# Two transformer blocks in one kernel: orders, waits and small products at the passages between stages

## What is computed

```python
def first_block(x, ...):
    x = x + 0.5 * swiglu(rmsnorm(x, g_ffn1), w1_gate, w1_up, w1_down)      # ffn1, 2816 hidden
    p = rmsnorm(x, g_mix) @ w_in
    qa, ka, va, qi, ki, wi, cq, ckv, kr = jnp.split(p, split_points, axis=-1)
    ...                                # rotary positions on qa, ka, qi, ki and parts of cq, kr
    out_a = dsa_sparse_attention(qa, ka, va, qi, ki, wi)     # top 128 keys chosen by an index score
    out_b = mla_attention(cq, ckv, kr, ...)                  # latents normed, then 8 causal heads
    x = x + jnp.concatenate([out_a, out_b], axis=-1) @ w_out
    x = x + 0.5 * swiglu(rmsnorm(x, g_ffn2), w2_gate, w2_up, w2_down)      # ffn2
    return rmsnorm(x, g_final)

def second_block(x, c, ctx, c_ctx, ...):
    ml = jnp.split(silu(c) @ w_mod + b_mod, 9)               # modulation of x
    mc = jnp.split(silu(c_ctx) @ w_mod + b_mod, 9)           # and of the context
    x = x + 0.5 * ml[2] * swiglu_2(modulate(rms_norm(x, norm1_g), ml[0], ml[1]), ...)   # ffn3
    cx = cx + 0.5 * mc[2] * swiglu_2(modulate(rms_norm(cx, norm1_g), mc[0], mc[1]), ...)
    ...                                # norm2, w_in_2: convolution branch, 8 query and 2 key heads
    x = x + ml[5] * merge_branches(y_conv, o_l, gates, w_branch_conv, w_branch_attn, w_out)
    x = x + 0.5 * ml[8] * swiglu_2(modulate(rms_norm(x, norm3_g), ml[6], ml[7]), ...)   # ffn4
    return rms_norm(x, final_g)
```

## Time and profile before

| | us |
|---|---|
| median of 3 runs | 2712.87 |
| lowest and highest | 2710.14, 2714.3 |
| profiled execution, whole | 2712.72 |
| its span from the first to the last instruction | 2710.9 |

### The profile page before, as it was taken

How to read it: one execution, slowest core, us unless ns; L and a number is a source line. 1 busy time by engine, 2 the same in 40 slices (tenths; PEclk the granted TensorE clock), 3 DMA queues, 4 the chain that set the end, 5 groups by cost and what they waited for, 6 DMA issues and landing times.

```text
span 2710.9 us, 32788 instructions
## 1 busy us (share of the span) xinstructions
PE 2637.7 (97%) x12170; PEld 2105.8 (78%) x12170; DVE 1332.3 (49%) x2039; ACT 758.4 (28%) x1035; POOL 372.5 (14%) x274
## 2 busy tenths in 40 slices
PE   8999999998999999999999999999999999999998
PEld 6888877754468888878888888888887658888887
DVE  7666674577647665572222222444226653433334
ACT  4111132255622221241111111323322452321223
POOL 2111120000012010142102102202000003210102
PEclk9999999889899999999999999999999999999999
DMA  6444443200054444432122121232332002233331
GB/s 189 140 140 144 140 127 77 57 16 1 1 155 139 139 140 140 128 103 64 63 62 62 62 62 51 59 108 78 93 112 68 16 1 93 78 100 93 102 89 66
DMA packets 358031, 241.18 MB, mean 89 GB/s; under 512 B 14768, under 2 KB 356144, under 8 KB 357936
## 3 DMA queue, kind: packets, MB, share of 16 engines
q1 hardware_dynamic: 357936, 239.92, 30.0%
HBM read 237.79 MB, written 2.10 MB: 88 GB/s over the span
## 4 chain that ended last, share of the span: by engine, by line
PE 90%; DVE 4%; ACT 3%; issue 1%; DMA 1%; POOL 0%; SPq 0%; DVEq 0%; ACTq 0%; POOLq 0%
PE PS L716 23%; PE PS L723 22%; PE PS L718 22%; PE PS L698 4%; PE PS L701 4%; PE PS L699 4%; PE PS L1121 2%; PE PS L1101 1%; PE PS L895 1%; PE PS L977 1%; PE PS L970 1%; PE PS L950 1%; PE PS L655 1%; DVE VA L1501 1%; PE PS L1112 1%
## 5 line engine op out<-in xcount | busy, mean ns | idle before, releaser
L716 PE MATMUL PS<-NH,WH 128*128 128x512 f32 (+1 forms) x2128 | 621.1, 373 | 10.7 <-DVE WL L1477 3.8
L718 PE MATMUL PS<-NH,WL 128*128 128x512 f32 (+1 forms) x2128 | 619.0, 372 | 0.0
L723 PE MATMUL PS<-NL,WH 128*128 128x512 f32 (+1 forms) x2128 | 590.7, 372 | 0.0
L1477 DVE TENSOR_TENSOR WL<-RAW,WH 128x2048 fp32r<-128x2048 f32 x190 | 468.7, 2467 | 106.7 <-ACT WH L1149 106.3
L1149 ACT ACTIVATE WH<-RAW 128x2048 fp32r<-128x2048 f32 x190 | 363.8, 1915 | 527.9 <-PE PS L723 494.2
L716 PEld LDWEIGHTS PS<-NH,WH 128*128 128x128 f32 x2128 | 386.4, 188 | 82.6 <-issue 9.8
L723 PEld LDWEIGHTS PS<-NL,WH 128*128 128x128 f32 x2128 | 388.9, 189 | 72.0 <-POOL NL L2076 0.4
L718 PEld LDWEIGHTS PS<-NH,WL 128*128 128x128 f32 x2128 | 388.6, 188 | 71.6
L1223 ACT ACTIVATE SA<-PS 128x512 f32<-128x512 f32 x104 | 62.2, 599 | 628.9 <-PE PS L723 595.6
L716 PE MATMUL PS<-HH,WH 128*128 128x512 f32 (+1 forms) x820 | 238.1, 371 | 0.0
L718 PE MATMUL PS<-HH,WL 128*128 128x512 f32 (+1 forms) x820 | 237.8, 371 | 0.0
(11 more groups left out here) (305 smaller groups left out, 2602.0 us busy)
## 6 DMA issues: line engine op xcount, KB each, us to landing
RAW<-in_ffn_w_in SPq DMA_DIRECT2D x88, 512.0 KB, 5.0
MW<-in_w_mod SPq DMA_DIRECT2D x72, 512.0 KB, 3.5
RAW<-in_w_in SPq DMA_DIRECT2D x70, 512.0 KB, 4.4
RAW<-in_w_gate SPq DMA_DIRECT2D x44, 512.0 KB, 4.1
RAW<-in_w_up SPq DMA_DIRECT2D x44, 512.0 KB, 5.3
RAW<-in_w_down SPq DMA_DIRECT2D x32, 512.0 KB, 4.4
RAW<-in_ffn_w_out SPq DMA_DIRECT2D x32, 512.0 KB, 4.0
RAW<-in_w_out SPq DMA_DIRECT2D x16, 512.0 KB, 4.5
```

What stands on the lines that cost most here:

```text
L716: pe.matmul(outs[half][x], w[half][0], xh(k), start=k == 0, stop=False)
L718: pe.matmul(outs[half][x], w[half][1], xh(k), start=False, stop=False)
L723: last = pe.matmul(outs[half][x], w[half][0], xl(k), start=False, stop=k == kn - 1)
L1477: dve.tensor_tensor(WL[1 - s][:, :], RAW[1 - s][:, :], WH[1 - s][:, :].bitcast(F32), ALU.subtract).then_inc(w_lo, 1)
```

## The change

- Norms: the diagonals go. The inverse root itself, a column read 128 times (`spread`), is the stationary operand and `ident` the moving one. This holds for the final norm of the first block too, where GpSimd made the diagonals.
- w_in: the weights of stage 1 are asked for ahead of the constants, and VectorE's wait for the constants stands behind the first split.
- Tail stages: VectorE adds the first half's residual ahead of the split.
- Modulation: the last four stages of ffn1, the stages of `w_out` and the last two chunks of ffn2 carry none; 30 stages of ffn3 do, with sums in CXIN. The fold has three parts in place of two, and its last is finished behind the convolution.
- w_out and w_branch_attn: the first stage begins with the four k that are ready and waits for `at_o` (`at2_o`) in its middle. SyncE waits for `at_o` only before the context's loads.
- First attention: the mask instruction gives the negated value and its minimum, so the negation goes and exp takes scale -1. From unit 48 on VectorE multiplies in place of ScalarE.
- The memset before the convolution clears the two edge columns alone.

```diff
-        M0 = {"ffn1": 0, "wo": NF + 12, "ffn2": NF + 12 + KD // 2}
-        assert M0["ffn2"] + NF + 12 == 2 * MOD_PAIRS
+        M0 = {"ffn1": 0, "ffn2": NF + 8, "ffn3": NF + 20}
         NCTX = 5 * KD
...
+        def last_mods(name, c):
+
+            return {("ffn1", 2): 1, ("ffn3", 2): 1, ("ffn2", 0): 2}.get((name, c), 0)
...
+        def spread(r, t):
+
+            return r[:, t:t + 1].to_broadcast([P, P])
...
+        BY_ACT = 48
...
                             sp.dma_start(MW[t][:, :, :], mod_weights(t, 0)).then_inc(mod_loaded[t], 16)
                     return
                 t = (s + b0) % 2
-                if m0 == M0["wo"]:
-                    sp.wait_ge(at_o, NG)
                 if not (isinstance(j, int) and j + m0 < 2):
                     sp.wait_ge(mod_s, j * 8 + 8 * (m0 - 1))
...
-                if n == 0:
+                if n == 1:
                     sp.wait_ge(pe_done, w_in_b)
-                    sp.wait_ge(mod_s, 8 * M0["wo"])
+                    sp.wait_ge(mod_s, 8 * M0["ffn2"])
                     for dst, src in ((TA, "rope64"), (TB, "rope96")):
...
                         .then_inc(w_loaded[s], 16)
-            pairs(wo_b, KD // 2, inp["w_out"][0], 0, KD, 0, m0=M0["wo"])
+            pairs(wo_b, KD // 2, inp["w_out"][0], 0, KD, 0)
+            sp.wait_ge(at_o, NG)
             for t in range(TC // P):
...
                     busy(4)
+                pe.wait_ge(norm_dg, m.dg + m.cols)
                 for t in range(m.cols):
-                    pe.wait_ge(norm_dg, m.dg + t + 1)
-                    pe.matmul(norm_bank(m)[:, t * P:(t + 1) * P], ones[:, :], diagonal(m, t), start=True, stop=True)\
+                    pe.matmul(norm_bank(m)[:, t * P:(t + 1) * P], spread(roots(m), t), ident[:, :], start=True, stop=True)\
                         .then_inc(norm_bc, 1)
...
+            def tiles(outs, wt, xs, kn, ready=None, m=None, within=None, halves=None):
+
+                ks = list(range(kn))
+                if halves is not None:
+                    ks = ks[halves[0]:] + ks[:halves[0]]
+                for i, k in enumerate(ks):
+                    if halves is not None and i == KD // 2:
+                        pe.wait_ge(*halves[1])
                     if within and k == kn - 2:
                         within()
                     if m is not None:
...
-                pe.wait_ge(at_r, u + 1)
+                if u < BY_ACT:
+                    pe.wait_ge(at_r, u + 1)
+                else:
+                    pe.wait_ge(at_q, u + 1 - BY_ACT)
...
-            pe.wait_ge(at_o, NG)
-            pairs(wo_b, KD // 2, XS, xb, KD, straight=True, m0=M0["wo"])
+            pairs(wo_b, KD // 2, XS, xb, KD, straight=True, halves=(KD // 2, (at_o, NG)))
             norm(norm2, ffn2[0][0])
...
-            fold(MOD_EARLY, ZCOLS, 2 * MOD_PAIRS, G[1 - ffn3[0][0] % 2])
+            fold(MOD_EARLY, 16 * BOTH, M0["ffn3"], G[1 - ffn3[0][0] % 2])
...
             ffn(ffn3, norm_x1, H0["ffn3"], XCS, HCS, xcb)
             norm(norm_x2, conv_b)
+            fold(16 * BOTH, ZCOLS, 2 * MOD_PAIRS, B[4])
             gate_up(conv_b, KD, XS, xb, None, m=norm_x2)
...
-            pe.wait_ge(at2_o, KVC * NT)
-            pairs(ba_b, KD // 2, XS, xb, KD)
+            pairs(ba_b, KD // 2, XS, xb, KD, straight=True, halves=(0, (at2_o, KVC * NT)))
...
-                act.activation(p, p, ACT.Exp, bias=stat(NM, u), accum_out=stat(DEN, u))\
+                act.activation(p, p, ACT.Exp, bias=stat(NM, u), scale=-1.0, accum_out=stat(DEN, u))\
...
-                if 0 <= u + 1 < len(UNITS):
+                if 0 <= u + 1 < BY_ACT:
...
-            def norm_diagonal(m):
-                own.settle(dve, dve.reciprocal(roots(m), roots(m)))
-                for t in range(m.cols):
-                    dve.tensor_scalar(diagonal(m, t), ident[:, :], roots(m)[:, t:t + 1], None, ALU.mult)\
-                        .then_inc(norm_dg, 1)
+                norm_reciprocal(m)
+
+            def norm_reciprocal(m):
+                dve.reciprocal(roots(m), roots(m)).then_inc(norm_dg, m.cols)
...
-                    if lead:
+                    if lead and b0 != ffn3[0][0]:
                         mods(b0, j, s, m0)
                     if low is not None:
                         norm_low(low, j)
                     if b0 == ffn3[0][0] and isinstance(j, int) and j == 0:
                         final_applied()
+                        mods(b0, j, s, m0)
                     dve.wait_ge(gate_done, j + (g0 + 1))
...
+                    tail = isinstance(b, int) and b in TAILS
                     mods(b0, j, s, m0)
-                    if at is not None:
+                    if at is not None and not tail:
                         split(s, b)
-                    tail = isinstance(b, int) and b in TAILS
...
                     for half, bank in enumerate((G, U)):
                         if tail and half:
+                            if at is not None:
+                                split(s, b)
                             dve.wait_ge(pe_done, b + 1)
...
-            dve.wait_ge(a_loaded, 64)
-            own.settle(dve, dve.memset(VAP[:, :, :, :], 0.0))
             for n in range(10):
                 b = w_in_b + n
                 s = b % 2
                 split(s, b)
+                if n == 0:
+                    dve.wait_ge(a_loaded, 64)
+                    own.settle(dve, dve.memset(VAP[:, :, :, :], 0.0))
...
-                own.inc(dve.tensor_tensor_reduce(out=p_slot(u)[:, 0:keys], in0=B[u % 2][:, 0:keys], in1=bias,
-                                                 scale=scale, scalar=3 * NEG * 1e7, op0=ALU.add, op1=ALU.max,
-                                                 accum_out=stat(NM, u)))
-                return own.n
-
-            def negated(u, n):
-                dve.wait_ge(dve_s, n)
-                dve.tensor_scalar(stat(NM, u), stat(NM, u), -1.0, None, ALU.mult).then_inc(at_m, 1)
+                dve.tensor_tensor_reduce(out=p_slot(u)[:, 0:keys], in0=B[u % 2][:, 0:keys], in1=bias,
+                                         scale=-scale, scalar=-3 * NEG * 1e7, op0=ALU.add, op1=ALU.min,
+                                         accum_out=stat(NM, u)).then_inc(at_m, 1)
 
             def inverse(u):
                 dve.wait_ge(at_e, u + 1)
-                dve.reciprocal(stat(DEN, u), stat(DEN, u)).then_inc(at_d, 1)
+                if u < BY_ACT:
+                    dve.reciprocal(stat(DEN, u), stat(DEN, u)).then_inc(at_d, 1)
+                else:
+                    p = p_slot(u)[:, 0:(UNITS[u][2] + 1) * P]
+                    own.settle(dve, dve.reciprocal(stat(DEN, u), stat(DEN, u)))
+                    dve.tensor_scalar(p, p, stat(DEN, u), None, ALU.mult).then_inc(at_q, 1)
...
-                n = masked(u + AHEAD) if u + AHEAD < len(UNITS) else None
+                if u + AHEAD < len(UNITS):
+                    masked(u + AHEAD)
                 if u >= 0:
                     next(selection, None)
-                if n is not None:
-                    negated(u + AHEAD, n)
-                if u >= 0:
                     if u % PER_GROUP == 1 and u > 1:
...
-            dve.memset(VA[:, :, 0:T + 2], 0.0).then_inc(conv_s, 1)
+            dve.memset(VA[:, :, 0:T + 2:T + 1], 0.0).then_inc(conv_s, 1)
...
+            dve.wait_ge(mod_folded, 3)
+            own.settle(dve, folded(BOTH, MOD_PAIRS, 1))
+            mods_finished(2 * BOTH, NMOD * KD, (4,), HALVED[2:3])
             dve.wait_ge(conv_s, 3 * KD + 1)
...
-            pool.wait_ge(f_r, 1)
-            for t in range(NT):
-                pool.tensor_scalar(FD[:, t * P:(t + 1) * P], ident[:, :], RF[:, t:t + 1], None, ALU.mult).then_inc(f_dg, 1)
```

More of the change, by code:

```diff
@@ L702, in tile @@
                 return last
-            def tiles(outs, wt, xs, kn, ready=None, m=None, within=None):
-                for k in range(kn):
+            def tiles(outs, wt, xs, kn, ready=None, m=None, within=None, halves=None):
[5 more added lines that the diff above has]
+                        pe.wait_ge(*halves[1])
                     if within and k == kn - 2:
@@ L722, in tiles @@
                         for half in range(2):
-                            last = pe.matmul(outs[half][x], w[half][0], xl(k), start=False, stop=k == kn - 1)
+                            last = pe.matmul(outs[half][x], w[half][0], xl(k), start=False, stop=i == kn - 1)
                 return last
@@ L798, in pairs @@
                     else:
-                        last = tiles((banks[0][s], banks[1][s]), wt, xs, kn, ready)
+                        last = tiles((banks[0][s], banks[1][s]), wt, xs, kn, ready,
+                                     halves=halves if isinstance(j, int) and j == 0 else None)
                     last.then_inc(pe_done, 1)
```

108 lines of the change are left out of this document (51 added, 57 removed).

## The result

The changed kernel takes 2681.8 us (median of 4 runs, 2679.98 to 2684.41) against 2712.3 us before: 30.5 us less, a ratio of 0.9888 with a 95% interval of 0.9871 to 0.9906. The profiled execution of the change has a span of 2677.9 us, 33.0 less than the 2710.9 of before.

The account below looks back on a forecast made before the run. TensorE (PE), busy 97% of the span, was taken as the bound. Terms of 0.2, 7.7, 5.8, 4.5, 1.6 and 0.9 us summed to 20.7, taking 2712.7 to 2692 us, range 2682 to 2701.

Parts of the forecast that it names:

- What bounds the kernel: Whole kernel: TensorE (PE) busy 97% of the span; only places where it stands still or runs at lower clock can give.
- Passage into w_in, 7.7: ffn1's end into w_in: 5.94 us from the earlier weight DMA, 1.25 from the first k, 0.49 from a split wait.
- Roots, 0.2: Norms: dropping the diagonals saves 0.2 us at the kernel's start, nothing where warm-ups stand ahead; column load costs no more.
- rival (b): Less gain: slower spread, VectorE bound at attention's end, second clock fall; 2700 us, chance 0.10.
- First attention, 5.8: First attention: 3.0 us from dropping the negation, 0.4 and 2.4 from moving the last 16 units' normalisation to VectorE.
- Rival (a): More gain: PE keeps the upper clock in the first attention, some 10 us more; 2681 to 2685 us, chance 0.14.
- The prediction's own sign of being wrong: First attention: the prediction called itself wrong if this moved by under 2 or over 12 us.
- Into w_out and w_branch_attn, 4.5: Ahead of both projections: PE's waits of 1.41 and 1.69 us for low halves and 1.45 for a weight tile go.
- End of ffn2, 1.6: Passage at norm_x1: ScalarE's squares start 1.24 us earlier, plus 0.3; PE's wait for GpSimd stays, longer than 2.4 us.
- norm_x2, 0.85: Ahead of the convolution: VectorE's memset of 0.92 us shrinks to two columns, saving 0.85 us.
- Range: Whole kernel: 2682 to 2701 us, from summing the upper and lower ends of all terms.
- the upper ends: Each term's largest gain (0.3, 8.7, 12.5, 4.7, 3.6, 0.9), together 30.7 us less, 2682 us.

Follow-up runs that it names:

- the twin: The changed kernel, unaltered, run and profiled a second time as yardstick for the other kernels: 2680.7 us, ratio 0.9885 to the kernel before.

## Why the prediction was wrong, step by step

- **What bounds the kernel**: right as to place; inside ffn3 PE stays full. Wrong as to currency. I read that only places where PE "stands still or runs at the lower granted clock can give", and then priced standing still at every place and the clock at one, `w_in`. Of 33.0 us 21.2 were busy time, and some 19 (56.9 less 37.5) is what the mean clock alone accounts for.
- **Passage into w_in, 7.7**: right, 8.8 measured. The passage shrank by 7.20 (13.18 to 5.98) and not 5.94, since its clock didn't fall; in the twin it fell, and 6.3 would have been measured, so the extra part is a draw. The first k took 1.46 us (1.24 less, 1.25 forecast), and the split's 0.49 gave 0.3. The order alone gave 6.3 in the trace.
- **Roots, 0.2**: right that the diagonals are hidden at the warmed-up norms. At the start 0.9 between the two traces, 0.6 to 0.8 for the edit alone, and not 0.2. The column as stationary operand costs no more: at the full clock, in `w_in`'s passage, the spread took 1.06 us with it and 1.16 with the diagonals put back; at the lower clock 1.91 both before and in the kernel with SyncE's order undone. That rules out the slower spread of rival (b).
- **First attention, 5.8**: the step that failed. Undone together the edits cost 12.7, done alone they gave 11 to 12. What failed is not the waits: at equal clock they are worth an estimated 3.0 us for the negation and 2.2 for the normalisation, where I had 3.0 and 2.8. It is the clock, which this term put at nothing: it took PE's busy time in the attention as fixed ("PE's own 9.16 is then the bound"), and that time fell by 11.6 us between the two traces. The neighbours' loads were off as well: in the change's last head products ScalarE is busy 8.54 us and not 6.7, VectorE 6.20 and not 7.4. Why the clock falls less often with the edits stays open; the trial with warm-ups in the holes did not reproduce it. The prediction's own sign of being wrong came true: the attention moved by over 12 us, 14.8 with the 1.4 ahead of `w_out`. Rival (a) named this and its time, 2681 to 2685, which is where the kernel is; I gave it 0.14 with the selection on VectorE against it. The rows at hand said more: the clock was 0.83 over 123 us, and PE full at half its pace is a bound that disappears when the clock rises. A part is luck: the trace that I priced against had the longest attention of its four.
- **Into w_out and w_branch_attn, 4.5**: the 1.41, 1.45 and 1.69 us all went; undone, the two halves cost 4.7 (8.4 by the ratios) where their terms are 3.1. In the traces it is 2.0 at `w_out`, and 1.9 at `w_branch_attn` between before and change; the difference to 4.7 is within the interval.
- **End of ffn2, 1.6**: 2.1 measured, and its bound held: the 2.1 us of the split went, PE's wait for GpSimd stayed and is longer (2.63 against 2.40), as the blocked add moved with the split. But it came from the modulation that left, not from the new order, without which the passage is 1.0 us shorter still in the trace.
- **norm_x2, 0.85**: 1.4, of which the shorter memset can be 0.5 (the hole of 1.62 us became 1.09) and the passage itself 0.6, at a clock of 0.80 in place of 0.64; in the second execution of the kernel before it was 0.80 too, so that part is a draw. The end of the convolution (clock 0.71 to 0.84 over 11.90 and 10.57 us) and norm_x3 (0.84 to 1.00) gave 2.5 us that no term had; no run tied these to an edit, and the clock there moved between executions too.
- **Range**: the upper ends summed to 2682 with every one of them reached. An end that leaves out what the clock can give in a stretch is not an end.

## What to carry over

Price PE's time in two currencies: the holes that an edit closes, and the busy time in stretches below the full clock, which can shrink by up to half. The two can't be told apart by adding up busy and idle time, since a slow PE fills its own holes: compare stretches in which both traces have the same clock. A stretch where PE is "busy" at 0.54 of its clock is not bound by PE in the sense in which a full stretch at 1.00 is. Where one execution of one kernel differs from the next by 4 us in a stretch, the sum should be made against two executions, and a gain of 2 us in a hole is not safe until the matmuls behind it have been looked at.

## What the runs showed of the hardware that was not expected

- The same instructions in the same order, from the first to the last product of the attention, took 170.96 us in one execution and 166.98 in another, PE's busy time 149.10 and 143.41.
- At a granted clock of 0.54 to 0.55, 28 matmuls kept PE busy for 10.6 to 10.8 us of 11.0 to 11.4; at 1.00 the same took 6.29 busy in 8.26. PE stood still for 0.35 to 0.6 us in the first case and for 1.97 in the second.
- With both edits in place and no instruction of the attention changed, an edit 200 us ahead went with 0.54 in place of 1.00 for these 28 matmuls.
- A hole that was 2.0 us shorter was followed by 30 matmuls that took 7.00 in place of 5.32 us.
- A weight load of one column read 128 times showed no price of its own: eight records of the spread in 1.06 us, 1.16 with ordinary operands, both at 1.00.
